# Operand tiles of a two-block transformer kernel begin at 128 instead of 192 modulo 256 bytes

## What is computed

```
x = x + 0.5 * swiglu_ffn(x)                     # width 2816
h = rms_norm(x); aq..cg, gates = split(h @ w_in)
y_a, y_b, y_c = diff_attention, chunk_attention, retention
merged = sum_i sigmoid(gates_i) * (y_i @ w_branch_i)
x = x + merged @ w_out
x = x + 0.5 * swiglu_ffn(x)
```

## Time and profile before

| | us |
|---|---|
| median of 3 runs | 1930.31 |
| lowest, highest | 1926.91, 1937.6 |
| the profiled execution | 1912.12 |
| its span, first to last instruction | 1910.3 |
| mean granted TensorE clock in it | 0.96 |

### The profile page before, as it was taken

How to read it: one execution, slowest core, us unless ns; L and a number is a source line. 1 busy time by engine, 2 the same in 40 slices (tenths; PEclk the granted TensorE clock), 3 DMA queues, 4 the chain that set the end, 5 groups by cost and what they waited for, 6 DMA issues and landing times.

```text
span 1910.3 us, 29373 instructions
## 1 busy us (share of the span) xinstructions
PE 1729.7 (91%) x13004; PEld 1625.2 (85%) x13004; DVE 1297.0 (68%) x1422; ACT 927.9 (49%) x1009; POOL 192.9 (10%) x72
## 2 busy tenths in 40 slices
PE   5999999999999999999999899998685779679997
PEld 5999878989999999998799899997474667569997
DVE  4666677776766676667766677665888567746665
ACT  4545646653545555455566545444332435335453
POOL 0000000000000000000000000001443506510000
PEclk9999999999999999999999999999897889789999
DMA  5555544334455545565343346556221315225552
GB/s 200 180 191 211 201 156 173 111 133 171 160 199 198 188 173 194 211 221 177 138 150 132 137 163 235 195 199 220 91 86 59 118 44 220 88 89 188 191 196 89
DMA packets 44622, 309.15 MB, mean 162 GB/s; under 512 B 5200, under 2 KB 5968, under 8 KB 7632
## 3 DMA queue, kind: packets, MB, share of 16 engines
q1 hardware_dynamic: 43632, 306.49, 44.6%
q10 hardware_dynamic: 864, 0.80, 0.1%
HBM read 306.22 MB, written 1.05 MB: 161 GB/s over the span
## 4 chain that ended last, share of the span: by engine, by line
PE 71%; DVE 17%; ACT 5%; DMA 4%; issue 2%; POOL 0%; ACTq 0%; DVEq 0%
PE ps L790 19%; PE ps L792 18%; PE ps L791 18%; DMA raw<-in_w_dram 3%; DVE wlo L1280 3%; PE ps L886 2%; PE ps L888 2%; PE ps L887 2%; ACT whi L451 2%; DVE pre L1778 2%; PE ps L1086 2%; PE ps L1074 1%; DVE pre L1781 1%; PE ps L900 1%; DMA decay<-in_decay_dram 1%
## 5 line engine op out<-in xcount | busy, mean ns | idle before, releaser
L451 ACT ACTIVATE whi<-raw 128x2048 fp32r<-128x2048 f32 x285 | 543.9, 1915 | 555.6 <-DMA raw<-in_w_dram 555.5
L1280 DVE TENSOR_TENSOR wlo<-raw,whi 128x2048 fp32r<-128x2048 f32 x257 | 586.7, 2289 | 222.8 <-ACT whi L451 220.6
L790 PE MATMUL ps<-h1hi,whi 128*128 128x256 f32 x1792 | 502.0, 280 | 26.7 <-DMA decay<-in_decay_dram 19.6
L791 PE MATMUL ps<-h1hi,wlo 128*128 128x256 f32 x1792 | 499.0, 278 | 0.0
L792 PE MATMUL ps<-h1lo,whi 128*128 128x256 f32 x1792 | 499.0, 278 | 0.0
L790 PEld LDWEIGHTS ps<-h1hi,whi 128*128 128x128 f32 x1792 | 339.8, 190 | 28.7 <-DMA decay<-in_decay_dram 19.6
L791 PEld LDWEIGHTS ps<-h1hi,wlo 128*128 128x128 f32 x1792 | 339.6, 189 | 0.1
L792 PEld LDWEIGHTS ps<-h1lo,whi 128*128 128x128 f32 x1792 | 339.4, 189 | 0.0
L790 PE MATMUL ps<-hid_hi,whi 128*128 128x256 f32 x880 | 244.7, 278 | 8.9 <-DVE hid_lo L1280 8.9
L792 PE MATMUL ps<-hid_lo,whi 128*128 128x256 f32 x880 | 244.5, 278 | 0.0
L791 PE MATMUL ps<-hid_hi,wlo 128*128 128x256 f32 x880 | 244.4, 278 | 0.0
(11 more groups left out here) (290 smaller groups left out, 2854.9 us busy)
## 6 DMA issues: line engine op xcount, KB each, us to landing
raw<-in_w_dram SPq DMA_DIRECT2D x285, 1024.0 KB, 4.8
relbias<-in_relbias_dram SPq DMA_DIRECT2D x2, 1024.0 KB, 6.9
pv<-in_pv_dram SPq DMA_DIRECT2D x2, 641.0 KB, 6.0
xT<-in_x_dram SPq DMA_DIRECT2D x4, 256.0 KB, 3.6
ctxT<-in_ctx_dram SPq DMA_DIRECT2D x1, 1024.0 KB, 6.9
out_dram<-xT SPq DMA_DIRECT2D x4, 256.0 KB, 2.5
decay<-in_decay_dram ACTq DMA_DIRECT2D x1, 512.0 KB, 14.2
dft_tok<-in_dft_tok_dram SPq DMA_DIRECT2D x1, 512.0 KB, 7.7
```

What stands on the lines that cost most here:

```text
L451: act.activation(whi[:, slot, :], raw[:, slot, :], ACT.Copy).then_inc(hi_done[slot], 1)
L790: pe.matmul(out, w_hi, hi, start=start, stop=False, skip_group_check=skip)
L791: pe.matmul(out, w_lo, hi, start=False, stop=False, skip_group_check=skip)
L1280: return dve.tensor_tensor(out, a, b, op)
```

## The change

`operand_base` pads to 128 modulo 256 in place of 192, and the two asserts follow.

```diff
     def operand_base():
 
-        base[0] += (192 - base[0]) % 256
+        base[0] += (128 - base[0]) % 256
         return base[0]
...
     for first in (hhi0, g0, a0, c0, t0, base[0]):
-        assert first % 256 == 192, first
+        assert first % 256 == 128, first
...
     v0 = base[0]
-    assert v0 % 256 == 192
+    assert v0 % 256 == 128
```

## The result

| | before | changed |
|---|---|---|
| median, us | 1928.61 (4 runs) | 1958.37 (4 runs) |
| lowest to highest, us | 1925.44 to 1937.6 | 1955.66 to 1961.47 |
| the profiled execution, us | 1912.12 | 1955.66 |
| its span, us | 1910.3 | 1953.9 |
| granted clock | 0.960 | 0.959 |

The ratio of the mean times is 1.0147 (of the medians 1.0154), with a 95% interval of 1.0109 to 1.0186: the changed kernel is slower by about 1.5%, 30 us. Each ratio further down is against executions of the kernel before that were taken beside that experiment, and one execution of the first experiment, 1945.15 us at a clock of 0.952, is left out of its ratio.

The account below looks back on a forecast made before the run. The prediction took TensorE's matmul stream as the bound and summed 0 + 0 + 0 against the profiled 1912.1 us, but forecast on the runs' median: 1930 us, no measurable change (0.37), range 1888 to 1982 us.

Parts of the forecast that it names:

- my first rival: New address relation puts TensorE's matmuls on the 117.8 ns step or worse: +43 us, 1973 us; chance of slower 0.35.
- What bounds the kernel: TensorE's stream of matmuls sets the time; starts in the FFNs lie 113.3 ns apart.
- the ruler: For 256-wide matmuls, recorded duration less 163 ns gives the time from one start to the next.
- the value I take is 0, by the transposes: 256-wide matmuls, activations moving: no change, as transposes 128 and 0 apart both take 272 or 273 ns; ends -21 to +38 us.
- That 128 lies between 64 and 192 for the 512-wide form: Input projections and `ada` would lose 2 ns more each (+2 us), `hx` as much less (-0.5 us); taken as 0.
- The long step as the upper bound: 256-wide matmuls: at worst all 8,400 steps of 113.3 ns become 117.8 ns, +38 us.
- My +43 us: Price of the slower case everywhere: +38 us from 256-wide matmuls and +5 us from 512-wide ones, giving 1973 us.
- Executions differ by more than the effects priced here; the short step's share may be part of it: Runs' median 1930.3 lies 18 us above the profiled execution; how many stretches step by 113.3 ns may partly explain it.
- The rest at nothing: Vector, Scalar, GpSimd work and weight slabs cost nothing, hidden under TensorE: 4.8 us issue to landing against 5.44 us a slab.
- Rival 2: 128 is the best relation: 117.8 ns steps vanish, 512-wide matmuls lose their excess; -42 us, 1888 us; chance of faster 0.28.

Follow-up runs that it names:

- the first experiment: Changed kernel with the weight ring also moved up 192 bytes (activations at 128, weights at 192), against the kernel before: 1928.1 us, ratio 1.0018.
- The second profile: The kernel before, unchanged, profiled once more: 1923.94 us, span 1922.2, against 1912.12 and 1910.3 the first time.

## Why the prediction was wrong

I forecast 1930 us and no measurable change; it is 1958 us, inside the stated range, and the case is my first rival, which had 0.35. By the test that the prediction set itself, 88 matmuls in 10 us of an FFN to within 1%, it is wrong too: there are 84.5.

- **What bounds the kernel** was right. The whole difference is in TensorE's step, and the ruler (duration less 163 ns is the step) held to within 1 ns in the changed kernel: 281 ns for 118.7.
- **The step that failed is "the value I take is 0, by the transposes".** It put the largest term of the sum, the 256-wide matmuls, at nothing; their mean step went from 114.1 to 118.7 ns, 47 us. The transposes had the relation in question, 128 for `score1` and 0 for `qkC`, but they are plain fp32. How slow that is stood on the trace of before, in the sums of squares (moving `sq` past `ones`):

```profile
L799 PE MATMUL ps<-sq,ones x24: 377/378/381, 33.0 to 1145.2; 128*128 128x256 f32 x24
```

378 ns is a step of 215 ns for 256 columns, twice the 106.7 of the fp32r form's columns. By that rate a transpose's 128 columns alone take 107 of its 109 ns. So "can only be paced by their weight loads" was not shown for the transposes (the 64-wide ones at 112 ns bear it out), and what sets them apart is that they stream at half the rate. They read 272 ns in the changed kernel as well, which is no second test: `ident`, `score1` and `qkC` moved together and keep their distances. I had written that they were no proof and then let them decide. For fp32r matmuls at the full clock, distances of 64 and 192 were both on the trace, 5 ns apart in the 512-wide form. That row was of the right kind and said that the distance matters.
- **That 128 lies between 64 and 192 for the 512-wide form was right**: 232.4 and 232.3 ns, from 229.2 and 233.4, though nearer to the longer one, which cost 3 us where I took 0. The same reading should have made me expect a change in the 256-wide form too. Since 1 ns of its step is 0.55% of the kernel, no measurable change required it to stay within 1 ns, which is a narrow case.
- **The long step as the upper bound** was nearly the size: 117.8 for a measured 118.7 ns. It is another pattern, though. My +43 us on the profiled 1912 would have given 1955, and that profile took 1955.7, which is partly luck: I added up 38 and 5, and measured are 47 and 3, less 6 of idle time. I put the 43 us on the median instead, 1973, as if it, too, had the first profile's 17% of long steps. The second profile shows 47% of them; the median execution had already paid part of the price. The sum had to be made against the profiled execution, and then compared by what the two kernels' executions have in common.
- **"Executions differ by more than the effects priced here; the short step's share may be part of it"** was right, and more than a part: 11.9 us of span for 3,003 long steps.
- **The rest at nothing** held: VectorE, ScalarE and GpSimd within 2.2 us, and 4.8 us from issue to landing for a slab, as in the earlier trace rows.
- **Rival 2**, that half a period is the best place, fell. Distance 192 is the best of the seven measured for the 256-wide form. What is left of its reasoning is the bound: in no stretch of any kernel did this form's mean go below 113 ns.
- The Trainium skill's N/2.4 + 2.5 ns ("TensorE: Matmul & The Clock Gate", "Back-to-back issue gap") and its sentence that PE never waits on anyone ("SBUF — State Buffer", "SBUF: two separate sides") do not describe this stream: the measured step is 113.3 to 120.0 ns against 109.2, and it depends on where the two operands lie to each other. The prediction also left out that the section gives the formula for an isolated matmul; for a stream of loads and matmuls it gives about 131 ns at 512 columns, and here that form steps by 227.3 to 234.2 ns. Measurement decides.

## What to carry to other kernels

Where fp32r matmuls run back to back at the full clock with a weight load each, the start of the moving tile relative to the start of the weights, modulo 256 bytes, is a tuning parameter. In this kernel it is worth up to 6% of the step (113.3 to 120.0 ns) and 2.4% of the time; pin both addresses, and measure the multiples of 64 in the shape at hand, because the best distance for one width (192 for 256 columns) is not the best for another (0 for 512). Read the count of matmuls in a window without waits, not the durations alone, and look at more than one profile: two executions of one kernel differed by 12 us, by the count of long steps mostly through the pattern into which each FFN fell. And where a row is to stand for an unseen case, prefer the row that streams at the same rate to the one with the same geometry.

## What the runs showed of the hardware

- Neither operand's place counts alone: activations at 128 with weights at 0, and activations at 192 with weights at 64, give 845 matmuls in 100 us alike, and moving both operands together gives back the kernel before.
- The steps lock into patterns that hold for a whole FFN of some 150 us: 885 or 852 matmuls in 100 us at distance 192, 855 or 835 at 160, and in the traces taken one single pattern each at 0 (835), 64 (851) and 128 (845).
- What counts is the moving tile's address less the stationary one's, in both roles: with activations at 160 (weights at 0) `hx` steps by 234.2 and the projections, at distance 96, by 233.5 ns; with activations at 96 it is 233.4 and 234.2.
- At the lower clock the loss is absent: 427 ns for 512 columns at 1.2 GHz, and by my count over the starts a median of 213 ns for 256 columns, the columns alone, in every kernel of this case, whatever the distance.
- Plain fp32 streams at half the rate of fp32r (215 ns for 256 columns) and shows 272 to 275 ns for 64 and 128 columns at distances 0 and 128; those of the earlier trace rows were seen at no other distance. What the memory does when the two streams meet is not visible in any of these traces; that they hinder each other is inferred from the steps.
